# Third layer of a three-block network: the low parts of its weights from GpSimd to VectorE, interleaved with the convolution halves

## The reference: what is computed

```python
h = rmsnorm(x, norm_mix_g)
proj = h @ w_in          # 1024 x 11784
q_m, k_m, v_m, if_pre, o_pre, q_a, k_a, v_a, gate_pre = split(proj)
qk  = silu(causal_depthwise_conv([q_m, k_m], conv_w, conv_b))   # 4 taps
lf  = log_sigmoid(if_pre[4:] + b);  ig = if_pre[:4] + b         # gates of the memory
hm  = mlstm_cell(q_m, k_m, v_m, ig, lf)                         # 4 heads of 256
hm  = (hm - mean) * rsqrt(var + EPS);  y_a = sigmoid(o_pre) * hm
y_b = dilated attention over q_a, k_a, v_a                      # 24 heads of 64
x   = x + (sigmoid(gate) mix of y_a @ w_proj_a, y_b @ w_proj_b) @ w_out
x   = x + (silu(hf @ w_gate) * (hf @ w_up)) @ w_down
```

## Time and profile before

| | |
|---|---|
| median of 3 runs | 1229.12 us |
| the profiled execution: its own time / its span | 1223.58 / 1221.8 us |
| TensorE busy | 1154.1 us (94%) |
| VectorE, ScalarE, GpSimd busy | 646.6, 600.0, 209.8 us |
| TensorE clock granted, mean | 0.977 of full |
| TensorE's share of the chain that ended last | 70% |
| hardware queue: 182.33 MB | 46.0% of the 16 DMA engines |

### The profile page before, as it was taken

How to read it: one execution, slowest core, us unless ns; L and a number is a source line. 1 busy time by engine, 2 the same in 40 slices (tenths; PEclk the granted TensorE clock), 3 DMA queues, 4 the chain that set the end, 5 groups by cost and what they waited for, 6 DMA issues and landing times.

```text
span 1221.8 us, 18852 instructions
## 1 busy us (share of the span) xinstructions
PE 1154.1 (94%) x7581; PEld 1044.6 (85%) x7581; DVE 646.6 (53%) x942; ACT 600.0 (49%) x781; POOL 209.8 (17%) x118
## 2 busy tenths in 40 slices
PE   8999999999889999999999949989899999999997
PEld 8768999998778899999888849988788988999996
DVE  5663655555678365555424354475445572555554
ACT  5573644444777364444444335535565445444343
POOL 3543100001473400000367610000000004000000
PEclk8999999999998999999999979999899999999999
DMA  8827465564433256555545525346433344665552
GB/s 235 265 86 186 158 210 189 175 203 139 128 108 105 69 173 207 180 198 173 172 144 168 175 83 159 104 152 219 129 108 117 106 141 146 196 206 192 180 177 86
DMA packets 138459, 193.92 MB, mean 159 GB/s; under 512 B 7083, under 2 KB 112776, under 8 KB 138396
## 3 DMA queue, kind: packets, MB, share of 16 engines
q1 hardware_dynamic: 127148, 182.33, 46.0%
q10 hardware_dynamic: 10640, 10.64, 3.1%
q0 software_dynamic: 608, 0.08, 0.0%
HBM read 191.90 MB, written 6.37 MB: 162 GB/s over the span
## 4 chain that ended last, share of the span: by engine, by line
PE 70%; DVE 9%; ACT 8%; DMA 6%; POOL 4%; issue 2%; SPq 1%; ACTq 0%; DVEq 0%; POOLq 0%
PE psum L536 21%; PE psum L538 21%; PE psum L537 21%; POOL wlo L1508 4%; DMA raw<-in_w_in 4%; ACT whi L1533 3%; ACT arena L1519 3%; DMA raw<-in_a_w_in 2%; DVE wlo L2080 2%; PE psum L1221 1%; PE psum L625 1%; PE psum L1246 1%; DVE psum L2446 1%; PE psum L1081 1%; PE psum L1241 1%
## 5 line engine op out<-in xcount | busy, mean ns | idle before, releaser
L1533 ACT ACTIVATE whi<-raw 128x2048 fp32r<-128x2048 f32 (+2 forms) x175 | 327.3, 1872 | 286.2 <-PE psum L538 126.8
L2080 DVE TENSOR_TENSOR wlo<-raw,whi 128x2048 fp32r<-128x2048 f32 (+1 forms) x133 | 302.6, 2277 | 237.1 <-ACT whi L1533 236.9
L536 PE MATMUL psum<-xA,whi 128*128 128x256 f32 (+1 forms) x1352 | 389.3, 288 | 23.6 <-DVE wlo L2080 17.3
L537 PE MATMUL psum<-xA,whi 128*128 128x256 f32 (+1 forms) x1352 | 385.0, 285 | 0.0
L538 PE MATMUL psum<-xA,wlo 128*128 128x256 f32 (+1 forms) x1352 | 384.8, 285 | 0.0
L1508 POOL TENSOR_TENSOR wlo<-raw,whi 128x2048 fp32r<-128x2048 f32 (+2 forms) x72 | 182.4, 2556 | 806.3 <-ACT whi L1533 805.9
L536 PEld LDWEIGHTS psum<-xA,whi 128*128 128x128 f32 (+1 forms) x1352 | 261.2, 193 | 30.5 <-DVE wlo L2080 17.9
L537 PEld LDWEIGHTS psum<-xA,whi 128*128 128x128 f32 (+1 forms) x1352 | 261.4, 193 | 1.5
L538 PEld LDWEIGHTS psum<-xA,wlo 128*128 128x128 f32 (+1 forms) x1352 | 261.1, 193 | 0.1
L536 PE MATMUL psum<-whi,xC 128*128 128x512 f32 (+1 forms) x384 | 149.8, 390 | 5.8 <-POOL wlo L1508 3.4
L537 PE MATMUL psum<-wlo,xC 128*128 128x512 f32 (+1 forms) x384 | 149.1, 388 | 0.0
(11 more groups left out here) (265 smaller groups left out, 1230.7 us busy)
## 6 DMA issues: line engine op xcount, KB each, us to landing
raw<-in_w_in SPq DMA_DIRECT2D x42, 1024.0 KB, 5.2
raw<-in_mlp_w_up SPq DMA_DIRECT2D x32, 1024.0 KB, 5.4
raw<-in_mlp_w_down SPq DMA_DIRECT2D x32, 1024.0 KB, 4.9
raw<-in_w_gate SPq DMA_DIRECT2D x11, 1024.0 KB, 5.3
raw<-in_w_up SPq DMA_DIRECT2D x11, 1024.0 KB, 5.3
raw<-in_w_down SPq DMA_DIRECT2D x11, 1024.0 KB, 5.0
raw<-in_a_w_in SPq DMA_DIRECT2D x6, 1024.0 KB, 7.2
raw<-in_a_w_o SPq DMA_DIRECT2D x4, 1024.0 KB, 4.9
```

The source lines that it names most:

```text
L536: nc.tensor.matmul(out, lh, rh, start=start, stop=False, skip_group_check=skip)
L537: nc.tensor.matmul(out, lh, rl, start=False, stop=False, skip_group_check=skip)
L1533: nc.scalar.activation(whi[c % N_SPLIT][:, 0:n], raw[c % N_RAW][:, 0:n], ACT.Copy).then_inc(hi_sem, 1)
L2080: V.tensor_tensor(wlo[c % N_SPLIT][:, 0:n], raw[c % N_RAW][:, 0:n], f(whi[c % N_SPLIT][:, 0:n]), ALU.subtract).then_inc(lo_sem["dve"], 1)
```

## The change

Four things. (1) The low parts of `vm1a` to `km3` go to VectorE; on GpSimd stay `vm0a` and `vm0b`. (2) VectorE's and ScalarE's lists are interleaved by hand: the convolution is split into its two tiles, one low part stands behind each; the gate strips stand behind convolution 6, L2525 behind the first half of convolution 7, and the low parts of `qa4`, `qa5` and `ka0` go ahead of the gate scans. (3) The memory tail is cut into pieces, with the PSUM copies of `ka1` to `ka4` (and the low parts ahead of them) between; ScalarE's high part of `ka3` goes ahead of the last head's tail. (4) `C.rs` goes behind `vm0b` on TensorE.

```diff
@@ chunks
-    SLOT, "dve" if name == "va" else "pool")
+    SLOT, "pool" if (name, j) == ("vm", 0) else "dve")
...
-    add("if", [...], KT * 36)
+    add("if", [...], KT * 36, "dve")
-    cols(f"{'qm' if tile < 4 else 'km'}{tile % 4}", w_in2, ..., 256)
+    cols(f"{'qm' if tile < 4 else 'km'}{tile % 4}", w_in2, ..., 256, lo="dve")
@@ tensor
 token_part("vm0", 0, (2, 3), late_tile("C"))
+token_part("vm0", 1, (2, 3), late_tile("C"))
 out = open_bank("C.rs", 0)
...
-token_part("vm0", 1, (2, 3), late_tile("C"))
@@ scalar
-ahead("vm0a")
+split_to("vm1a")
...
 token_copy("vm0")
-ahead("qm0")
-ahead("vm1a")
-ahead("qm1")
-silu(0)
...
-silu(7)
-ahead("qa4")
+split_to("qm1")
+for c in range(8):
+    at = index["qm0"] + 2 * c
+    split_to(at + 3)
+    if c == 7:
+        act.wait_ge(*done["C.e1"])
+        run(C["g"][:, 0, :], C["g"][:, 0, :], ACT.Ln, done["C.ln"])
+    silu(c, 0)
+    if c < 7:
+        split_to(at + 4)
+    if c in (1, 3, 5):
+        token_copy({1: "vm1", 3: "o0", 5: "o1"}[c])
+    silu(c, 1)
+    if c == 6:
+        act.wait_ge(*read["if.0"])
+        run(C["g"][:, 0, :], C["gT"][:, 1, :], ACT.Abs)
+        run(C["g"][:, 0, :], C["g"][:, 0, :], ACT.Exp, done["C.exp"], scale=-1.0)
 for blk in range(NB):
     run(C["so"][:, blk, :], C["so"][:, blk, :], ACT.Sigmoid, done["C.so"] if blk else None)
+split_to("qa0")
 act.wait_ge(*done["C.mrow"])
 run(C["g"][:, 0, :], C["g"][:, 0, :], ACT.Exp, done["C.em"])
-ahead("qa5")
 ahead("ka0")
...
-    ahead(f"qa{h}")
+    ahead(f"qa{h}" if h < M_HEADS - 1 else "ka1")
@@ vector
-next_low = [index["qa4"]]
+next_low = [index["qm0"]]
...
+low_to(index["qm1"])
+dve.wait_ge(*read["C.rs"])
+for c in range(8):
+    at = index["qm0"] + 2 * c
+    conv(c, 0)
+    if c == 7:
+        dve.wait_ge(*done["C.exp"])
+        run(V.tensor_scalar(g[:, 0, :], g[:, 0, :], 1.0, None, ALU.add), done["C.e1"])
+    low_to(at + 3)
+    conv(c, 1)
+    if c == 6:
+        gate_rows()
+    if c < 7:
+        low_to(at + 4)
 dve.wait_ge(*done["C.ln"])
...
-for h in range(M_HEADS):
-    for blk in range(NB):
-        c = blk * 4 + h
-        x = C["hm"][:, blk, h * 256:h * 256 + 256]
-        run(V.tensor_scalar(x, x, mmu[:, c:c + 1], mvar[:, c:c + 1], ALU.add, ALU.mult))
-dve.wait_ge(*done["C.so"])
-for blk in range(NB):
...
-for j in range(1, 6):
-    attention_copy(f"ka{j}")
+hidden_normed((0, 1))
+attention_copy("ka1")
+hidden_normed((2, 3))
+attention_copy("ka2")
+dve.wait_ge(*done["C.so"])
+hidden_gated(0)
+attention_copy("ka3")
+hidden_gated(1)
+attention_copy("ka4")
+attention_copy("ka5")
```

More of the change, by code:

```diff
@@ L246, in program @@
             if tile == 7:
-                add("if", [(0, KT, 36, 0, 4, w_in2[:, :, C_IF:C_IF + 4]), (0, KT, 36, 4, 32, w_in2[:, :, C_IF - 24:C_IF + 8])], KT * 36)
-            cols(f"{'qm' if tile < 4 else 'km'}{tile % 4}", w_in2, (C_Q if tile < 4 else C_K) + 256 * (tile % 4), 256)
+                add("if", [(0, KT, 36, 0, 4, w_in2[:, :, C_IF:C_IF + 4]), (0, KT, 36, 4, 32, w_in2[:, :, C_IF - 24:C_IF + 8])], KT * 36, "dve")
+            cols(f"{'qm' if tile < 4 else 'km'}{tile % 4}", w_in2, (C_Q if tile < 4 else C_K) + 256 * (tile % 4), 256, lo="dve")
         for name, j in [("qa", 4), ("qa", 5), ("ka", 0)] + [("qa", j) for j in range(4)] + [("ka", j) for j in range(1, 6)]:
@@ L1894, in _, with silu @@
                 run(sd[:, b:b + 1], ms[:, b:b + 1], ACT.Sqrt, done[f"C.sd{b}"])
-            ahead("vm0a")
+            split_to("vm1a")
             act.wait_ge(*full["C.rs"])
             run(row_scale, psum[:, bank["C.rs"], 0:SEQ], ACT.Copy, read["C.rs"])
[L1899 to L1904, removed]
+            def silu(c, nt):
+                tile = 2 * c + nt
+                name = f"{'qm' if c < 4 else 'km'}{c % 4}.0"
+                act.wait_ge(*(read[name] if nt else done[f"C.conv{tile}"]))
+                run(C["qk"][:, tile, :], C["acc"][:, nt, :], ACT.Silu, done[f"C.silu{tile}"])
             def token_copy(name):
-                ahead(f"{name}b")
                 j = int(name[-1])
@@ L1990, in _ @@
                 ahead(f"va{j}a")
+                ahead(f"va{j}b")
                 token_copy(f"va{j}")
@@ L2485, in _, with low_to @@
             rows2 = row_scale.unsqueeze(1).to_broadcast([P, 2, SEQ])
-            next_low = [index["qa4"]]
-            def low_ahead(name):
-                while next_low[0] <= min(index[name] + 2, index["co3"]):
+            next_low = [index["qm0"]]
+            def low_to(c):
+                while next_low[0] <= min(c, index["co3"]):
                     low_part(next_low[0], next_low[0] + 1)
                     next_low[0] += 1
[L2494 to L2514, removed]
@@ L2516, in _ @@
-            gT, g = C["gT"], C["g"]
[L2517 to L2524, removed]
@@ L2525, in _, with low_ahead, conv @@
-            run(V.tensor_scalar(g[:, 0, :], g[:, 0, :], 1.0, None, ALU.add), done["C.e1"])
-            conv(7)
+            def low_ahead(name):
+                low_to(index[name] + 2)
+            def conv(c, nt):
+                name, tile = f"{'qm' if c < 4 else 'km'}{c % 4}.0", 2 * c + nt
+                if nt == 0:
+                    dve.wait_ge(*full[name])
+                    both = bk(name, 0, 512).rearrange("p (a b) -> p a b", b=SEQ)
+                    run(V.tensor_tensor(both, both, rows2, ALU.mult))
+                if tile >= 2:
+                    dve.wait_ge(*done[f"C.silu{tile - 2}"])
+                x, acc = bk(name, nt * 256, nt * 256 + 256), C["acc"][:, nt, :]
+                run(V.tensor_scalar(acc, x, vec(V_CW + 48 + tile), vec(V_CB + tile), ALU.mult, ALU.add))
+                for tap in (2, 1, 0):
+                    d = 3 - tap
+                    then = None
+                    if tap == 0:
+                        then = read[name] if nt else done[f"C.conv{tile}"]
+                    run(V.scalar_tensor_tensor(acc[:, d:SEQ], x[:, 0:SEQ - d], vec(V_CW + 16 * tap + tile),
+                                               acc[:, d:SEQ], ALU.mult, ALU.add), then)
@@ new lines, in _, with gate_rows @@
+            gT, g = C["gT"], C["g"]
+            def gate_rows():
+                dve.wait_ge(*full["if.0"])
+                for i in range(2):
+                    src = psum[32 * i:32 * i + 4, bank["if.0"], 0:SEQ]
+                    run(V.tensor_tensor(gT[:, i, :], src, row_scale[32 * i:32 * i + 4, :], ALU.mult))
+                    run(V.tensor_scalar(gT[:, i, :], gT[:, i, :], gate_bias[0:4, i:i + 1], None, ALU.add),
+                        read["if.0"] if i else None)
+            low_to(index["qm1"])
@@ L2574, in _, with hidden_normed, hidden_gated @@
             run(V.reciprocal(mvar, mrstd))
-            for h in range(M_HEADS):
-                for blk in range(NB):
-                    c = blk * 4 + h
-                    x = C["hm"][:, blk, h * 256:h * 256 + 256]
-                    run(V.tensor_scalar(x, x, mmu[:, c:c + 1], mvar[:, c:c + 1], ALU.add, ALU.mult))
-            dve.wait_ge(*done["C.so"])
-            for blk in range(NB):
+            def hidden_normed(heads_):
+                for h in heads_:
+                    for blk in range(NB):
+                        c = blk * 4 + h
+                        x = C["hm"][:, blk, h * 256:h * 256 + 256]
+                        run(V.tensor_scalar(x, x, mmu[:, c:c + 1], mvar[:, c:c + 1], ALU.add, ALU.mult))
+            def hidden_gated(blk):
                 run(V.tensor_tensor(C["hm"][:, blk, :], C["hm"][:, blk, :], C["so"][:, blk, :], ALU.mult),
                     done["C.hn"] if blk else None)
-            for j in range(1, 6):
-                attention_copy(f"ka{j}")
+            hidden_normed((0, 1))
[8 more added lines that the diff above has]
+            attention_copy("ka5")
             for k in range(KT):
```

## The result

The changed kernel takes 1195.4 us, the median of 4 runs (1190.0 to 1199.6), against 1229.2 (1229.0 to 1232.1): ratio 0.9717, 95% interval 0.9675 to 0.9759. Two later measurements, each on one chip with 6 runs of the changed kernel and 11 of the other, gave 1195.9 against 1225.3 (0.9742, 0.9703 to 0.9781) and 1194.2 against 1222.2 (0.9767, 0.9736 to 0.9798): 29.4 and 28.0 us less. The forecast was 29.0 less.

A forecast was written before the change was run, and what follows sets the result against it. TensorE is busy nearly everywhere, so only its waits for GpSimd's and VectorE's low parts and `C.rs`, and slow clock behind longer pauses, could pay. Terms of 28.6 plus restarts made 29.0: 1229.1 to 1200.1 us, range 1197 to 1207.

The forecast's parts named there:

- the last step of the sum: Runs' median stays 5.5 us above the profiled execution (1223.6), so 1229.1 less 29.0 gives 1200.1 us.
- The waits of the forecast: TensorE's idle times in the third layer, before `C.rs`, every second chunk, `km3`, `qa4` and `ka3`, would go.
- the forecast had 4.4 for the clock: TensorE's slow clock behind longer pauses would go: 1.5 at `km3`, 1.6 behind `qa4`'s wait, 1.3 behind `ka3`'s.
- C.rs: TensorE's two waits for the scales before `C.rs` go once it stands behind `vm0b`: 0.65 + 0.71 = 1.4 us.
- The pairs: From `qm0` to `if`, each two chunks run at TensorE's 11.4 us instead of GpSimd's 11.8: 2.6 us gained.
- km3, then `qa4` to `ka0`: Waits for low parts before `km3` (4.4) and `qa4` (12.5) go, with slow clock behind them (1.5 and 1.6).
- Rival C: Low parts of `qa5` and `ka0` come late behind gate strips and Exp; 8 to 10 us stay, 1209; chance 0.08.
- The gate chain: ScalarE's silu, sigmoids and Exp reach `C.cols` at 722.4 with TensorE, no slack: 0 counted, ends 0 and 3 us.
- Rival A: ScalarE's gate chain is late at `C.cols`; 1203 at the bound of 3 us; chance 0.18.
- The heads: Memory heads behind `C.cols`: unchanged work, TensorE fully busy; last head's tail about 0.9 us later relative to TensorE.
- The memory tail: `ka3`'s low part ends 4.3 us earlier: 3.3 us of wait and 1.3 of slow clock gained, 0.3 wait stays.
- Rivals B and D: B (0.10): convolution halves stand in the slot ring, 1206. D (0.03): cross waits chain both slots, slower, 1236.

The follow-up runs named there:

- before_again: The kernel of before, no edit, measured again with a second trace: 1222.4 us (1218.9 to 1228.7, 12 runs).
- after_again: The changed kernel, no edit, measured once more for its spread: 1195.9 us (1193.0 to 1198.9, 6 runs).
- old_rs: The changed kernel with `C.rs` back between `vm0a` and `vm0b`: 1197.6 us (1187.7 to 1204.9).
- engine_only: The kernel of before with the low parts of `vm1a` to `km3` on VectorE, two behind each whole convolution, otherwise the old order: 1215.2 us (1208.7 to 1219.9).
- qa0_early: The changed kernel with ScalarE's high part of `qa0` between the halves of the last silu: 1191.7 us (1187.3 to 1193.4, 5 runs).

## Why the prediction was right about the change and wrong about the time

*What failed* is the last step of the sum: "The runs' median stands 5.5 us above that execution; I keep the distance". Three runs of before agreed within 0.2 us, and I took 1229.1 for a fixed property. In the later measurements, on four chips, 50 runs of it lie between 1217.6 and 1237.3, with a median of 1223.3: the profiled 1223.6 was the typical value, and the three runs were high. 1223.3 less 29.0 is 1194.3; the changed kernel's three medians are 1194.2 to 1195.9. So the 33.8 of the first comparison are, as far as this shows, 28 to 29 us of gain and some 5 of high runs of before. No clock of those runs is on record, so why they were high stays open. Besides, the range held only the bounds of the terms, and nothing for executions of one kernel that spread by 6 to 20 us.

*What the spread is.* For each run the time goes with the mean granted clock: 1223.1 at 0.977 and 1237.3 at 0.966 for before, 1190.0 at 0.987 and 1199.6 at 0.978 for the changed kernel. The median of time x clock is 1194 to 1195 in each of the four groups of before and 1173 to 1175 in the three of the changed kernel, so within one kernel the clock accounts for most of the spread (single products of before lie between 1191 and 1197, the times 20 us apart).

*Waits and clock apart.* The 20 us between these two products are not the avoided waits, because the mean clock also counts stretches in which TensorE stands idle and a low clock costs nothing: 0.61 over 715.00 to 727.40, with 0.00 us busy. The pages have the split. TensorE's idle time, span less busy, fell from 67.7 to 43.8 us between the first two traces and from 66.7 to 43.6 between before_again (1217.1 less 1150.4) and after_again (1193.3 less 1149.7): 23 to 24 us. The waits of the forecast, 1.4 + 2.1 + 4.4 + 12.5 + 3.3, make 23.7. The busy time fell by 9.7 us in the first pair of traces and by 0.7 in the second, because the lower clock falls elsewhere in each execution. Of the 28.0 to 29.4 us between the medians some 4 to 6 are then left for the clock and the restarts, an estimate; the forecast had 4.4 for the clock.

*The fixed part, term by term*, from the starts in the first two traces: forecast 29.0, measured 30.0.
- C.rs: 1.4 forecast. `vm0a` to `qm0` takes 11.4 instead of 13.6 us, 2.2; undone alone 1.9. What lies beyond the two brackets, 0.5 to 0.9 us, was not followed further.
- The pairs: 2.6 forecast, 4.1 measured, the most mis-sized term in these two traces. A pair takes 11.21 us (5.75 + 5.46), not 11.4: the 5.85 that I read off for a `qm` chunk held the restart of its first product, and the 5.55 for a token chunk part of the last product's tail. The waits alone were 2.1, and nearly as much again was hidden in the starts. It is no fixed term either: before_again needs 75.9 us from `qm0` to `if` against 77.2, which makes 2.8 measured.
- km3, then `qa4` to `ka0`: 4.4 + 1.5 + 12.5 + 1.6 = 20.0 forecast, and 0.45 for restarts. Measured 4.6 from `if` to `km3` and 15.4 from `km3` to `C.cols`, 20.0, and in that are 0.55 lost at `C.cols`. The low parts' times came out within 0.6 us of the listed ones, shifted by the shorter pairs: `qa4`'s from 696.6 to 698.9, 3.2 ahead of TensorE. Rival C did not occur.
- The gate chain: "no slack", 0 counted, 0.55 measured, 1.64 for 1.7 added. Rival A at a sixth of its bound. ScalarE's table loads take 1.28 us and the next operation starts 0.02 behind them in the rows above. The Trainium skill ("ScalarE: Activation LUTs", What ACT_TABLE_LOAD costs) has about 2.66 us with a drain; that rule's 5.5 us did not come, and the measurement decides.
- The heads: 0 forecast, a loss of 1.6 in this trace. This is the clock (0.84 from 720 to 731), where the prediction said 1.0 from 700 to 760. before_again has it too, so the change is not needed for it; whether the change makes it likelier stays open.
- The memory tail: 3.3 + 1.3 forecast, 5.4 measured, 5.6 when undone alone. The forecast left 0.3 us of wait at `ka3`; it is 0 here and 1.13 in old_rs. `ka3`'s low part ends 52.7 us behind `C.cols` in both; here the slow heads bring TensorE there 1.6 later. Before, it ended 55.15 behind `C.cols` (799.46 + 2.29 less 746.60), so it came 2.5 us earlier, where the forecast had 4.3 less 0.9. The slow heads thus cost 1.6 us and gave 1.4 back at `ka3` (29.0 us from `ka1` on against 30.4). VectorE's rows (2.29 us low part between 1.76 and 1.76 of normalising) answer to the earlier trace rows:

```profile
768.66 1.76 DVE L2579 TENSOR_SCALAR arena<-arena,st 128x256 f32<-128x256 f32 x4
770.46 2.29 DVE L2067 TENSOR_TENSOR wlo<-raw,whi 128x2048 fp32r<-128x2048 f32 x1
772.66 0.68 DVE L2544 TENSOR_TENSOR arena<-psum,scales 128x512 f32<-128x512 f32 x1
773.39 1.76 DVE L2579 TENSOR_SCALAR arena<-arena,st 128x256 f32<-128x256 f32 x4
```

Rivals B and D are out: neither in the changed kernel nor in engine_only does TensorE wait in the pairs.

*What stays open*: why the lower clock falls in the heads in one execution and not in the other; why the dilated attention takes 98.7 or 105 us, beyond that the clock falls there or does not; and why the first three runs of before were all at 1229.

## What to carry to other kernels

Anchor a forecast to an execution whose granted clock is known; a median of three equal runs says nothing of how the next ones spread, and the range has to hold that spread. A wait that recurs costs more than its brackets: compare the spacing with a stretch where nothing waits. When a wait on one engine's list is moved, follow the chunk whose load it lets go, not only the instruction behind it: the Exp moved forward gained 0.6 us at `C.cols` and made `ka3`'s low part 1.2 us later behind it, until the high part was put into idle time. And compare two traces only where the clock is the same in the stretch behind: of the 1.72 us in front of `ka3` with the Exp first, 1.13 stand in old_rs too, without that move.

## What the runs showed of the hardware that I had not expected

The lower clock level comes without a pause of TensorE nearby: in qa0_early TensorE was busy 99.00 of 99.00 us at 1.00 and then 41.23 of 41.23 us at a mean of 0.96. The stretch of the heads takes 39.7 us at 1.00 and 41.3 at 0.96 in the two executions of the kernel of before, and the same dilated attention 98.7 us at 1.00 and 103.5 at 0.95.

Slow heads cost almost nothing in the end, because the wait behind them shrank: with `ka3`'s low part 52.7 us behind `C.cols` in both, the changed kernel and old_rs take 70.3 and 70.1 us from `C.cols` to the transpositions, although the heads differ by 1.6.
